# Dense gate and up products with the weight slices as the stationary operand and all 256 tokens streaming

## The chip, the cores and the metric

The kernel runs on one core of a Trainium2 chip. The metric is the device time of one execution in microseconds (us). Three runs of the kernel before gave 1444.27 us as their median, from 1444.11 to 1446.06 us. TensorE (PE) has a granted clock that the profile shows as a share of 2.4 GHz.

## What is computed

A decoder trunk of two layers on 256 tokens with 1024 features: an mLSTM layer with a dense SwiGLU, then a latent attention layer with eight experts of which each token takes two. The change lies in the dense SwiGLU of the first layer:

```python
def swiglu(h, w_gate_up, w_down):
    g, u = jnp.split(h @ w_gate_up, 2, axis=-1)
    return (jax.nn.silu(g) * u) @ w_down

hf = rms_norm(x, ffn_norm[l])
x = x + swiglu(hf, dense_w_gate_up[l // 2], dense_w_down[l // 2])
```

Here `h` is 256 x 1024, `w_gate_up` 1024 x 7168 and `w_down` 3584 x 1024. The root mean square of a token is a factor of its row of `h`, so it may be applied behind the gate and up products. The gain of the norm is put on the normed side before them.

## The kernel before

All products are made in float32 as three passes of fp32r operands: each operand is split into a high part (a rounded copy, `whi`, `xhi`, `hhi`) and a low part (the rest, `wlo`, `xlo`, `hlo`), and high x high, high x low and low x high are summed in PSUM. ScalarE (ACT) makes the high parts of the weights from a ring of six slots in SBUF that SyncE's DMAs fill (`hi_of`), VectorE (DVE) makes the low parts (`lo_of`). Three cuts of split weights are held at a time (`CUTS`). A cut is 2048 columns wide on 128 partitions, and `through` counts the cuts that PE has finished with. `highs` and `lows` count the finished halves of the split.

The dense SwiGLU goes in `NB` = 14 blocks of 256 hidden features (`FB`). A block has two cuts of gate and up weights, one for each half of the 1024 input features (`gate_up`), and one cut of down weights (`down`). `gate_up` takes a slice of 128 features x 128 tokens of `xhi` or `xlo` as the stationary operand (`lhsT`) and streams 512 weight columns: 256 of gate, then 256 of up. With 8 slices of features, 2 tiles of tokens (`t`) and 3 passes that is 48 matmuls of 512 columns for a block, 24 for each cut. The result has tokens on the partitions, in two PSUM banks, one for each token tile. ACT then applies silu to the gate half with the token's factor `rx` as its scale (two instructions of 256 columns, into `sil`), and DVE multiplies the up half by `rx` and by `sil` (two instructions, into `hn`).

`down` needs the hidden features on the partitions. So `turn_hidden` makes four PE transposes of 128 x 128 for a block into a PSUM bank of their own, ACT copies them rounded into `hhi`, and DVE puts the rest into `hlo`. `down` then makes 24 matmuls of 512 columns that sum into PSUM banks 4 to 7.

The order of the work is written by hand, and each engine runs its own program in its order. On PE it is, for a block b in the loop: `gate_up(b)`, `down(b-1)`, `turn_hidden(b)`. Two blocks are one iteration of a hardware loop with five iterations, the first two and the last two blocks stand outside it. In the last block, the transposes stand in the middle of `down(12)`. On ACT and DVE, `block(b)` is: the split of the cuts of `cut_item(b)`, silu or the product, the split of the cut `next_item(b)`, then the split of the hidden features. In block 13 the split of `next_item` is that of the first cut of the next stage (`dkv.0`). `gate_up(0)` has an order of its own, pass by pass, since the normed rows arrive in four pairs of slices (`x1_high`, `x1_low`). On DVE a chain of small instructions for the rotary angles (from `posf` on) stands between `norm("x1")`, which gives `rx`, and block 0.

Of the kernel before, what the change touches and what calls it, by code (L numbers as in the profile page):

```python
# [18 lines left out]
ALU = mybir.AluOpType  # L19
# [7 lines left out]
P = 128  # L27
# [9 lines left out]
def build(nc, T, out):  # L37
# [117 lines left out]
    with ExitStack() as ctx:  # L155
# [108 lines left out]
        hn = carve(NT * FB, NT, FB)  # L264
        silE, hnE = carve(0, EB)[0:CAP], carve(NT * FB, EB)[0:CAP]
# [441 lines left out]
        def _(act):  # L707
# [47 lines left out]
            def block(b, r=None):  # L755

                for n in cut_item(b):
                    hi_of(n, r)
                act.wait_ge(S("through"), count(r, 3, FFN0 + gu_item(b) + 2))
                for t in range(NT):  # L760
                    last = nc.scalar.activation(sil[:, t], PS[:, gu_bank(b) + t, 0:FB], ACT.Silu, scale=rx[:, t:t + 1])
                last.then_inc(S("silu"), 1)
                if next_item(b) < PER:
                    hi_of(next_item(b), r)
                else:
                    front_hi(item["dkv.0"])
                act.wait_ge(S("h_turned"), count(r, 1, b + 1))
                nc.scalar.activation(hidden(b)[0], PS[:, turn_bank(b), :].rearrange("p (a s) -> p a s", a=2), ACT.Copy).then_inc(S("h_high"), 1)
# [146 lines left out]
            nc.scalar.activation(gt, gt, ACT.Exp, scale=-1.0).then_inc(S("gate_exp"), 1)  # L915
            act.wait_ge(S("gate_exp"), 1)
            nc.scalar.activation(gt, gt, ACT.Ln, bias=1.0).then_inc(S("gate_exp"), 1)
# [8 lines left out]
            nc.scalar.activation(gem, gm, ACT.Exp, scale=-1.0).then_inc(S("gate_em"), 1)  # L926
# [218 lines left out]
        def _(pe):  # L1145
# [182 lines left out]
            pe.wait_ge(S("gate_em"), 1)  # L1328
# [77 lines left out]
            def gate_up(b, r=None, between=None):  # L1406

                for h in range(2):
                    if h == 1 and between:
                        between()  # L1410
                    n = gu_item(b) + h
                    j = (FFN0 + n) % CUTS
                    if b == 0:
                        parts = [(k, h * KH + k, t, slice(t * P, (t + 1) * P)) for k in range(KH) for t in range(NT)]
                        pe.wait_ge(S("highs"), FFN0 + n + 1)
                        for k, kx, t, x_ in parts:
                            if k % 2 == 0 and t == 0:
                                pe.wait_ge(S("x1_high"), kx // 2 + 1)
                            mm(PS[:, t, :], lhsT=xhi[:, kx, x_], rhs=whi[:, j, k * W:(k + 1) * W], start=(kx == 0), stop=False)
                        pe.wait_ge(S("lows"), FFN0 + n + 1)  # L1420
                        for k, kx, t, x_ in parts:
                            mm(PS[:, t, :], lhsT=xhi[:, kx, x_], rhs=wlo[:, j, k * W:(k + 1) * W], start=False, stop=False)
                        for k, kx, t, x_ in parts:
                            if k % 2 == 0 and t == 0:
                                pe.wait_ge(S("x1_low"), kx // 2 + 1)
                            last = mm(PS[:, t, :], lhsT=xlo[:, kx, x_], rhs=whi[:, j, k * W:(k + 1) * W], start=False, stop=(kx == KD - 1))
                        last.then_inc(S("through"), 1)
                        continue
                    pe.wait_ge(S("lows"), count(r, 3, FFN0 + n + 1))
                    for k in range(KH):  # L1430
                        for t in range(NT):
                            x_ = slice(t * P, (t + 1) * P)
                            last = three(PS[:, gu_bank(b) + t, :], xhi[:, h * KH + k, x_], xlo[:, h * KH + k, x_], whi[:, j, k * W:(k + 1) * W],
                                         wlo[:, j, k * W:(k + 1) * W], h == 0 and k == 0, h == 1 and k == KH - 1)
                    last.then_inc(S("through"), 1)
# [50 lines left out]
            down(NB - 2, tiles=(1,))  # L1486
# [93 lines left out]
            pe.wait_ge(S("masks_r"), 4)  # L1580
# [200 lines left out]
        def _(dve):  # L1781
# [32 lines left out]
            def block(b, r=None):  # L1814

                for n in cut_item(b):
                    lo_of(n, r)
                dve.wait_ge(S("silu"), count(r, 1, b + 1))
                for t in range(NT):
                    last = v.scalar_tensor_tensor(out=hn[:, t], in0=PS[:, gu_bank(b) + t, FB:2 * FB], scalar=rx[:, t:t + 1], in1=sil[:, t],  # L1820
                                                  op0=ALU.mult, op1=ALU.mult)
                last.then_inc(S("h_ready"), 1)
                if next_item(b) < PER:
                    lo_of(next_item(b), r)
                else:
# [226 lines left out]
            dve.wait_ge(S("gate_exp"), 2)  # L2052
# [82 lines left out]
            norm("x1")  # L2135

# [307 lines left out]
```

## Time and profile before

| | |
|---|---|
| median of 3 runs | 1444.27 us |
| the profiled execution | 1444.03 us |
| its span (first to last instruction) | 1442.3 us |
| PE busy | 99% of the span |
| DVE busy | 79% |
| ACT busy | 67% |
| POOL (GpSimd) busy | 7% |
| dense SwiGLU, first matmul to the first transpose of the next stage | 139.97 to 375.13 us of the span |

The profile's times count from the first instruction. A matmul's row shows its start and a modelled end. Matmuls overlap in the array, so the time that one takes from the engine is read from the distance between starts. PEld is PE's weight load, which runs beside the matmul ahead of it.

### The profile page before, as it was taken

The numbers are of one execution on the slowest core, as the hardware profiler recorded it, in microseconds if no ns is written. First come the engines' busy times: TensorE is split into PE (matmuls) and PEld (weight loads), VectorE is DVE, ScalarE is ACT, GpSimd is POOL, SyncE is SP. The second block draws the span as 40 slices with busy tenths as digits, with TensorE's granted clock in tenths as the row PEclk, the third lists the DMA queues.
The fourth block names the chain that finished last, engine by engine and source line by source line (L and its number), as shares of the span: only waits on it lengthen the run. The fifth ranks groups of instructions, "written<-read, shape, count | busy, mean of one in ns | idle before, by whom it ended". The sixth has DMA issues, their size and how long they took to land.

```text
span 1442.3 us, 19828 instructions
## 1 busy us (share of the span) xinstructions
PE 1434.5 (99%) x6848; PEld 1206.7 (84%) x6848; DVE 1140.7 (79%) x896; ACT 963.9 (67%) x839; POOL 98.7 (7%) x146
## 2 busy tenths in 40 slices
PE   8999999999999999999999999999999999999999
PEld 8898888888998888888888888888888888888887
DVE  6566655454676599989888898898998898888897
ACT  7555443434694577777777777777777777777775
POOL 3010000000032110000000000000000000000100
PEclk9999999999999899999999999999999999999999
DMA  9534655554345599999999999999999999999995
GB/s 335 199 117 146 207 202 175 194 184 147 115 175 160 206 363 390 375 372 395 391 362 394 388 364 383 395 369 377 393 375 367 393 391 349 397 393 370 380 393 203
DMA packets 212591, 442.92 MB, mean 307 GB/s; under 512 B 16373, under 2 KB 56761, under 8 KB 212545
## 3 DMA queue, kind: packets, MB, share of 16 engines
q1 hardware_dynamic: 208640, 430.18, 82.1%
q0 software_dynamic: 3888, 12.13, 2.8%
q8 instruction: 28, 0.46, 0.1%
q14 instruction: 19, 0.15, 0.0%
q10 hardware_dynamic: 16, 0.00, 0.0%
HBM read 434.88 MB, written 7.37 MB: 307 GB/s over the span
## 4 chain that ended last, share of the span: by engine, by line
PE 99%; DVE 0%; ACT 0%; issue 0%; POOL 0%; POOLq 0%; DVEq 0%; ACTq 0%
PE PS L1698 21%; PE PS L1699 21%; PE PS L1702 21%; PE PS L1404 5%; PE PS L1402 5%; PE PS L1403 5%; PE PS L1149 4%; PE PS L1202 2%; PE PS L1197 2%; PE PS L1199 2%; PE PS L1253 1%; PE PS L1259 1%; PE PS L1256 1%; PE PS L1179 1%; PE PS L1687 1%; PE PS L1690 1%
## 5 line engine op out<-in xcount | busy, mean ns | idle before, releaser
L1844 DVE TENSOR_TENSOR wlo<-ring,whi 128x2048 fp32r<-128x2048 f32 x334 | 764.1, 2292 | 96.4 <-ACT whi L784 94.4
L784 ACT ACTIVATE whi<-ring 128x2048 fp32r<-128x2048 f32 x334 | 640.5, 1919 | 186.5 <-PE PS L1702 175.3
L1698 PE MATMUL PS<-whi,xhi 128*128 128x512 f32 x864 | 340.8, 394 | 0.0
L1699 PE MATMUL PS<-whi,xlo 128*128 128x512 f32 x864 | 336.6, 390 | 0.0
L1702 PE MATMUL PS<-wlo,xhi 128*128 128x512 f32 x864 | 231.0, 389 | 0.0
L1702 PEld LDWEIGHTS PS<-wlo,xhi 128*128 128x128 f32 x864 | 162.1, 188 | 33.9 <-DVE wlo L1844 0.2
L1699 PEld LDWEIGHTS PS<-whi,xlo 128*128 128x128 f32 x864 | 162.4, 188 | 32.4
L1698 PEld LDWEIGHTS PS<-whi,xhi 128*128 128x128 f32 x864 | 162.3, 188 | 32.4
L1698 PE MATMUL PS<-whi,hhi 128*128 128x512 f32 x440 | 171.9, 391 | 0.0
L1699 PE MATMUL PS<-whi,hlo 128*128 128x512 f32 x440 | 171.3, 389 | 0.0
L1811 DVE TENSOR_TENSOR wlo<-ring,whi 128x2048 fp32r<-128x2048 f32 x42 | 96.2, 2291 | 59.0 <-ACT whi L753 59.0
L1702 PE MATMUL PS<-wlo,hhi 128*128 128x512 f32 x440 | 117.8, 390 | 0.0
L753 ACT ACTIVATE whi<-ring 128x2048 fp32r<-128x2048 f32 x42 | 80.5, 1916 | 46.3 <-PE PS L1404 37.8
L1702 PEld LDWEIGHTS PS<-wlo,hhi 128*128 128x128 f32 x440 | 82.6, 188 | 17.2
L1699 PEld LDWEIGHTS PS<-whi,hlo 128*128 128x128 f32 x440 | 82.6, 188 | 17.0
L1698 PEld LDWEIGHTS PS<-whi,hhi 128*128 128x128 f32 x440 | 82.6, 188 | 16.9
L1402 PE MATMUL PS<-whi,xhi 128*128 128x512 f32 x224 | 88.3, 394 | 0.0
L1404 PE MATMUL PS<-whi,xlo 128*128 128x512 f32 x224 | 87.3, 390 | 0.0
L1403 PE MATMUL PS<-wlo,xhi 128*128 128x512 f32 x224 | 87.2, 389 | 0.0
L809 ACT ACTIVATE arena<-PS 128x512 f32<-128x512 f32 x56 | 33.5, 599 | 46.2 <-PE PS L1702 46.2
L1977 DVE TENSOR_TENSOR wlo<-ring,whi 128x1536 fp32r<-128x1536 f32 (+4 forms) x28 | 49.3, 1771 | 14.7 <-ACT whi L842 14.7
L1149 PE MATMUL PS<-ident,arena 128*128 128x128 f32 (+3 forms) x378 | 55.7, 272 | 0.0
(377 smaller groups left out, 1586.8 us busy)
## 6 DMA issues: line engine op xcount, KB each, us to landing
ring<-in_moe_w_gate_up SPq DMA_DIRECT2D x448, 512.0 KB, 6.8
ring<-in_moe_w_down SPq DMA_DIRECT2D x224, 512.0 KB, 6.7
ring<-in_dense_w_gate_up SPq DMA_DIRECT2D x56, 512.0 KB, 4.2
ring<-in_dense_w_down SPq DMA_DIRECT2D x28, 512.0 KB, 4.2
ring<-in_a_w_in SPq DMA_DIRECT2D x12, 768.0 KB, 7.1
ring<-in_mem_w_kv SPq DMA_DIRECT2D x4, 1024.0 KB, 5.3
ring<-in_a_w_out SPq DMA_DIRECT2D x4, 1024.0 KB, 4.9
ring<-in_b_w_out SPq DMA_DIRECT2D x4, 1024.0 KB, 5.0
```

Of the source, the lines that this page charges most:

```text
L753: nc.scalar.activation(whi[:, (FFN0 + n) % CUTS, :], ring[:, h * SLOT:(h + 1) * SLOT], ACT.Copy).then_inc(S("highs"), 1)
L784: nc.scalar.activation(whi[:, j, :], ring[:, h * SLOT:(h + 1) * SLOT], ACT.Copy).then_inc(S("highs"), 1)
L1149: return nc.tensor.transpose(dst, src, ident[0:src.shape[0], 0:src.shape[0]])
L1402: mm(out_, lhsT=xh, rhs=wh, start=first, stop=False)
L1403: mm(out_, lhsT=xh, rhs=wl, start=False, stop=False)
L1404: return mm(out_, lhsT=xl, rhs=wh, start=False, stop=last)
L1698: mm(out_, lhsT=xh, rhs=whi[:, j, c0:c0 + HD], start=begin, stop=False)
L1699: mm(out_, lhsT=xl, rhs=whi[:, j, c0:c0 + HD], start=False, stop=False)
L1702: last = mm(out_, lhsT=xh, rhs=wlo[:, j, c0:c0 + HD], start=False, stop=end)
L1811: v.tensor_tensor(wlo[:, j, :], ring[:, h * SLOT:(h + 1) * SLOT], whi[:, j, :].bitcast(F32), ALU.subtract).then_inc(S("lows"), 1)
L1844: v.tensor_tensor(wlo[:, j, :], ring[:, h * SLOT:(h + 1) * SLOT], whi[:, j, :].bitcast(F32), ALU.subtract).then_inc(S("lows"), 1)
L1977: last = v.tensor_tensor(lo, src, hi.bitcast(F32), ALU.subtract)
```

## The change

Gate and up products: the stationary operand is now a slice of 128 features x 128 weight columns of `whi` or `wlo`, and all 256 tokens of `xhi` or `xlo` stream past it. A cut has 4 slices of features, gate and up (`g`), two halves of 128 columns (`c`) and three passes: 48 matmuls of 256 columns where there were 24 of 512. The result has hidden features on the partitions and tokens in the columns, gate in one PSUM bank and up in the other. `turn_hidden` and its four transposes are gone.

The factor `rx` is then needed along the columns. DVE makes two diagonal matrices with `rx` (`rx_diag`), PE multiplies them by a matrix of ones into PSUM behind `gate_up(0)`, and DVE copies the 256 columns into `rx_rows`. In a block, DVE multiplies gate and up from PSUM by `rx_rows` into SBUF (`gs`, `us`, one instruction of 512 columns each), ACT applies silu to `gs` (one of 512 columns), DVE multiplies the two (`hn2`, 512 columns), ACT copies the product rounded into `hhi` (from SBUF, and behind a wait for `down(b-1)`, which reads the same tile), and DVE puts the rest into `hlo`. `gate_up` waits for `h_ready` of the block before from block 2 on. In the last block but one, `down(12)` is in one piece. Three semaphores of the gates of the first layer are merged into `gate_in`.

```diff
@@ gate_up
+                    def out_of(g, c):
+                        return PS[:, gu_bank(b) + g, c * SEQ:(c + 1) * SEQ]
+
+                    parts = [(k, h * KH + k, g, c, slice(k * W + g * FB + c * P, k * W + g * FB + (c + 1) * P))
+                             for k in range(KH) for g in range(2) for c in range(2)]
...
+                    if h == 0 and b > 1:
+                        pe.wait_ge(S("h_ready"), count(r, 1, b))
                     pe.wait_ge(S("lows"), count(r, 3, FFN0 + n + 1))
-                    for k in range(KH):
-                        for t in range(NT):
-                            x_ = slice(t * P, (t + 1) * P)
-                            last = three(PS[:, gu_bank(b) + t, :], xhi[:, h * KH + k, x_], xlo[:, h * KH + k, x_], whi[:, j, k * W:(k + 1) * W],
-                                         wlo[:, j, k * W:(k + 1) * W], h == 0 and k == 0, h == 1 and k == KH - 1)
+                    for k, kx, g, c, w_ in parts:
+                        mm(out_of(g, c), lhsT=whi[:, j, w_], rhs=xhi[:, kx, :], start=(kx == 0 and c == 0), stop=False, skip_group_check=True)
+                        mm(out_of(g, c), lhsT=whi[:, j, w_], rhs=xlo[:, kx, :], start=False, stop=False, skip_group_check=True)
+                        last = mm(out_of(g, c), lhsT=wlo[:, j, w_], rhs=xhi[:, kx, :], start=False, stop=(kx == KD - 1), skip_group_check=True)
                     last.then_inc(S("through"), 1)
@@ PE's order
-            def turn_hidden(b, r=None):
-
-                pe.wait_ge(S("h_ready"), count(r, 1, b + 1))
-                for kk in range(2):
-                    for t in range(NT):
-                        last = tr(PS[:, turn_bank(b), kk * SEQ + t * P:kk * SEQ + (t + 1) * P], hn[:, t, kk * P:(kk + 1) * P])
-                last.then_inc(S("h_turned"), 1)
-
             gate_up(0)
+            pe.wait_ge(S("masks_r"), 4)
+            for t in range(NT):
+                last = mm(PS[:, 4, t * P:(t + 1) * P], lhsT=ones[:, :], rhs=rx_diag[:, t], start=True, stop=True)
+            last.then_inc(S("gains_t"), 1)
             pe.wait_ge(S("x1_low"), 4)
-            gate_up(1, between=lambda: turn_hidden(0))
+            gate_up(1)
             down(0)
-            turn_hidden(1)
             with pe.Fori(0, len(REST)) as r:
                 for b in (2, 3):
                     gate_up(b, r)
                     down(b - 1, r)
-                    turn_hidden(b, r)
             gate_up(NB - 2)
             down(NB - 3)
-            turn_hidden(NB - 2)
             gate_up(NB - 1)
-            down(NB - 2, tiles=(0,))
-            turn_hidden(NB - 1)
-            down(NB - 2, tiles=(1,))
+            down(NB - 2)
             down(NB - 1)
@@ DVE's block(b)
+                dve.wait_ge(S("through"), count(r, 3, FFN0 + gu_item(b) + 2))
+                for g, dst, done in ((0, gs, "g_scaled"), (1, us, "h_ready")):
+                    v.tensor_tensor(dst, PS[:, gu_bank(b) + g, :].rearrange("p (a s) -> p a s", a=2), over(rx_rows, 2), ALU.mult).then_inc(S(done), 1)
+                dve.wait_ge(S("h_ready"), count(r, 1, b + 1))
                 dve.wait_ge(S("silu"), count(r, 1, b + 1))
-                for t in range(NT):
-                    last = v.scalar_tensor_tensor(out=hn[:, t], in0=PS[:, gu_bank(b) + t, FB:2 * FB], scalar=rx[:, t:t + 1], in1=sil[:, t],
-                                                  op0=ALU.mult, op1=ALU.mult)
-                last.then_inc(S("h_ready"), 1)
+                v.tensor_tensor(hn2, us, sil2, ALU.mult).then_inc(S("h_turned"), 1)
@@ ACT's block(b)
-                act.wait_ge(S("through"), count(r, 3, FFN0 + gu_item(b) + 2))
-                for t in range(NT):
-                    last = nc.scalar.activation(sil[:, t], PS[:, gu_bank(b) + t, 0:FB], ACT.Silu, scale=rx[:, t:t + 1])
-                last.then_inc(S("silu"), 1)
+                act.wait_ge(S("g_scaled"), count(r, 1, b + 1))
+                nc.scalar.activation(sil2, gs, ACT.Silu).then_inc(S("silu"), 1)
...
+                if 0 < b < NB - 1:
+                    act.wait_ge(S("through"), count(r, 3, FFN0 + dn_item(b - 1) + 1))
+                nc.scalar.activation(hidden(b)[0], hn2, ACT.Copy).then_inc(S("h_high"), 1)
@@ DVE, between norm("x1") and the rotary angles
             norm("x1")
+            dve.wait_ge(S("scaled"), nidx["x1"] + 1)
+            for t in range(NT):
+                last = v.tensor_scalar(rx_diag[:, t], ident[:, :], rx[:, t:t + 1], None, ALU.mult)
+            last.then_inc(S("masks_r"), 1)
+            dve.wait_ge(S("gains_t"), 3)
+            then(v.tensor_copy(rx_rows, PS[:, 4, 0:SEQ]))
```

PE's program in the first block before: six passes of `gate_up(0)` (L1419 to L1426), then `gate_up(1)`.

```order
368 L1419 MATMUL PS<-whi,xhi 128x512 x8
369 L1422 MATMUL PS<-wlo,xhi 128x512 x8
370 L1426 MATMUL PS<-whi,xlo 128x512 x8
...
374 L1402 MATMUL PS<-whi,xhi 128x512
375 L1403 MATMUL PS<-wlo,xhi 128x512
376 L1404 MATMUL PS<-whi,xlo 128x512
```

The same place now. L1472 are the two products with the matrix of ones.

```order
368 L1425 MATMUL PS<-xhi,whi 128x256 x16
369 L1428 MATMUL PS<-xhi,wlo 128x256 x16
370 L1432 MATMUL PS<-xlo,whi 128x256 x16
...
374 L1472 MATMUL PS<-arena,ones 128x128 x2
375 L1439 MATMUL PS<-xhi,whi 128x256
376 L1440 MATMUL PS<-xlo,whi 128x256
377 L1441 MATMUL PS<-xhi,wlo 128x256
```

Each pass has twice the matmuls at half the width, the operands have changed sides, and two small matmuls stand between the blocks.

PE's program at the end of the hardware loop's iteration before: the last matmuls of `down`, then `turn_hidden` (L1149) and the branch back.

```order
599 L1402 MATMUL PS<-whi,hhi 128x512
600 L1403 MATMUL PS<-wlo,hhi 128x512
601 L1404 MATMUL PS<-whi,hlo 128x512
602 L1464 REGISTER_ALU
603 L1149 MATMUL PS<-ident,arena 128x128 x4
604 L1475 REGISTER_ALU
605 L1475 COMPARE_AND_BRANCH
```

The same place now.

```order
741 L1406 MATMUL PS<-whi,hhi 128x512
742 L1407 MATMUL PS<-wlo,hhi 128x512
743 L1408 MATMUL PS<-whi,hlo 128x512
744 L1477 REGISTER_ALU
745 L1477 COMPARE_AND_BRANCH
```

The four transposes are gone, and `down` is followed by the branch.

DVE's program before, from `rx` on (L1802) through the rotary angles to block 0 (from L1811 on; L1820 is the product into `hn`, L1828 the rest `hlo`).

```order
80 L1802 COPY rx<-rstd 128x2
81 L2147 CAST posf<-posi 128x2
82 L2149 TENSOR_SCALAR rot<-invf,posf 128x32 x2
...
90 L2160 TENSOR_SCALAR rot<-rot 128x64
91 L1811 TENSOR_TENSOR wlo<-ring,whi 128x2048
92 L1820 SCALAR_TENSOR_TENSOR arena<-PS,rx,arena 128x256 x2
93 L1811 TENSOR_TENSOR wlo<-ring,whi 128x2048
94 L1828 TENSOR_TENSOR hlo<-PS,hhi 128x512
```

The same place now (L2136 makes `rx_diag`, L2139 copies `rx_rows`, L1818 makes `gs` and `us`, L1821 `hn2`).

```order
80 L1800 COPY rx<-rstd 128x2
81 L2136 TENSOR_SCALAR arena<-ident,rx 128x128 x2
82 L2139 COPY arena<-PS 128x256
83 L2151 CAST posf<-posi 128x2
84 L2153 TENSOR_SCALAR rot<-invf,posf 128x32 x2
...
93 L1809 TENSOR_TENSOR wlo<-ring,whi 128x2048
94 L1818 TENSOR_TENSOR arena<-PS,arena 128x512 x2
95 L1821 TENSOR_TENSOR arena<-arena 128x512
96 L1809 TENSOR_TENSOR wlo<-ring,whi 128x2048
97 L1827 TENSOR_TENSOR hlo<-arena,hhi 128x512
```

Three instructions stand ahead of the rotary angles, one of which waits for PE, and a block has four instructions of 512 columns beside the splits, where it had two of 256 and one of 512.

## Rows read from the trace of the kernel before

**Rows 1.** The page: the span, and each engine's busy time, share and instructions.
```profile
span 1442.3 us, 19828 instructions
PE 1434.5 (99%) x6848; PEld 1206.7 (84%) x6848; DVE 1140.7 (79%) x896; ACT 963.9 (67%) x839; POOL 98.7 (7%) x146
```

**Rows 2.** Windows of the span: length, busy time by engine, clock, DMA share, GB/s.
```profile
139.97:375.13 235.16, 235.16 (x1066) 194.72 (x1065) 126.56 (x116) 103.25 (x103) 2.24 (x2) 1.00 0.54 178
...
471.00:481.30 10.30, 10.18 (x64) 9.47 (x62) 5.89 (x18) 4.54 (x8) 1.95 (x4) 0.79 0.33 127
```

**Rows 3.** Groups by line and form, PE, 139.9 to 375.13 us.
```profile
L1402 PE MATMUL PS<-whi,xhi 128*128 128x512 f32 x216 | 85.2, 395 | 0.0
...
L1149 PE MATMUL PS<-ident,arena 128*128 128x128 f32 x56 | 8.4, 272 | 0.0
L1419 PE MATMUL PS<-whi,xhi 128*128 128x512 f32 x16 | 4.1, 395 | 0.0
```

**Rows 4.** Timeline of PE, one block: start us, us, engine, line, operation, tiles.
```profile
224.70 0.39 PE L1402 MATMUL PS<-whi,xhi 128*128 128x512 f32 x1
...
234.90 0.60 PE L1149 MATMUL PS<-ident,arena 128*128 128x128 f32 x4
235.26 0.48 PE L1402 MATMUL PS<-whi,xhi 128*128 128x512 f32 x1
...
236.04 0.39 PE L1402 MATMUL PS<-whi,xhi 128*128 128x512 f32 x1
...
251.69 0.60 PE L1149 MATMUL PS<-ident,arena 128*128 128x128 f32 x4
```

**Rows 5.** Timeline of PE behind the dense stage: matmuls of 384, then 256 columns.
```profile
388.46 0.33 PE L1197 MATMUL PS<-whi,xhi 128*128 128x384 f32 x1
...
391.06 0.33 PE L1199 MATMUL PS<-whi,xlo 128*128 128x384 f32 x1
...
393.30 0.29 PE L1197 MATMUL PS<-whi,xhi 128*128 128x256 f32 x1
...
396.78 0.28 PE L1199 MATMUL PS<-whi,xlo 128*128 128x256 f32 x1
```

**Rows 6.** Timeline of PE: an output product whose matmuls share stationary slices in pairs.
```profile
466.88 1.07 PE L1253 MATMUL PS<-whi,xhi 128*128 128x512 f32 x4
...
469.60 1.03 PE L1149 MATMUL PS<-ident,xres 128*128 128x128 f32 x8
```

**Rows 7.** Timeline of DVE, then of ACT, then of PE in the first block.
```profile
148.40 0.17 DVE L1802 COPY rx<-rstd 128x2 f32<-128x2 f32 x1 [0.92 <-POOL rstd L613]
148.48 0.17 DVE L2147 CAST posf<-posi 128x2 f32<-128x2 int32 x1
...
151.53 2.28 DVE L1811 TENSOR_TENSOR wlo<-ring,whi 128x2048 fp32r<-128x2048 f32 x1
...
148.61 1.92 ACT L753 ACTIVATE whi<-ring 128x2048 fp32r<-128x2048 f32 x1 [2.72 <-DVE rx L1802]
...
139.97 2.08 PE L1419 MATMUL PS<-whi,xhi 128*128 128x512 f32 x8
```

**Rows 8.** Groups by line: elementwise instructions on 512 and 256 columns.
```profile
L1804 DVE TENSOR_TENSOR arena<-arena,rstd 128x512 f32<-128x512 f32 x3 | 2.1, 692 | 5.9 <-POOL rstd L613 5.9
...
L716 ACT ACTIVATE arena<-arena 128x512 f32<-128x512 f32 x1 | 0.6, 624 | 0.0
...
L2006 DVE TENSOR_SCALAR memv<-PS,rm 128x256 f32<-128x256 f32 x4 | 1.8, 480 | 3.5 <-ACT arena L859 3.5
```

**Rows 9.** Timeline of PE, ACT and DVE in the last block.
```profile
363.78 0.39 PE L1402 MATMUL PS<-whi,hhi 128*128 128x512 f32 x1
...
369.69 0.39 PE L1402 MATMUL PS<-whi,xhi 128*128 128x512 f32 x1
...
364.71 1.92 ACT L842 ACTIVATE whi<-ring,gains 128x320 fp32r<-128x320 f32 x4
...
366.65 1.94 DVE L1979 SCALAR_TENSOR_TENSOR wlo<-ring,gains,whi 128x320 fp32r<-128x320 f32 x4 [0.93 <-ACT whi L842]
```

More of the change, by code:

```diff
@@ L264, in build @@
         hn = carve(NT * FB, NT, FB)
+        gs, us = carve(2 * NT * FB, 2, SEQ), carve(3 * NT * FB, 2, SEQ)
+        rx_rows = carve(4 * NT * FB, SEQ)
+        rx_diag = carve(4 * NT * FB + SEQ, NT, P)
+        sil2, hn2 = carve(0, 2, SEQ), carve(NT * FB, 2, SEQ)
         silE, hnE = carve(0, EB)[0:CAP], carve(NT * FB, EB)[0:CAP]
@@ L767, in block @@
                 act.wait_ge(S("h_turned"), count(r, 1, b + 1))
-                nc.scalar.activation(hidden(b)[0], PS[:, turn_bank(b), :].rearrange("p (a s) -> p a s", a=2), ACT.Copy).then_inc(S("h_high"), 1)
+                if 0 < b < NB - 1:
+                    act.wait_ge(S("through"), count(r, 3, FFN0 + dn_item(b - 1) + 1))
+                nc.scalar.activation(hidden(b)[0], hn2, ACT.Copy).then_inc(S("h_high"), 1)
             def dense():
@@ L914, in _ @@
             act.wait_ge(S("gate_steps"), 1)
-            nc.scalar.activation(gt, gt, ACT.Exp, scale=-1.0).then_inc(S("gate_exp"), 1)
-            act.wait_ge(S("gate_exp"), 1)
-            nc.scalar.activation(gt, gt, ACT.Ln, bias=1.0).then_inc(S("gate_exp"), 1)
+            nc.scalar.activation(gt, gt, ACT.Exp, scale=-1.0).then_inc(S("gate_in"), 1)
+            act.wait_ge(S("gate_in"), 3)
+            nc.scalar.activation(gt, gt, ACT.Ln, bias=1.0).then_inc(S("gate_in"), 1)
             front_hi(7)
@@ L925, in _ @@
             act.wait_ge(S("gate_steps"), 2)
-            nc.scalar.activation(gem, gm, ACT.Exp, scale=-1.0).then_inc(S("gate_em"), 1)
+            nc.scalar.activation(gem, gm, ACT.Exp, scale=-1.0).then_inc(S("gate_in"), 1)
             front_hi(9)
@@ L1327, in _ @@
             pe.wait_ge(S("v_out"), 1)
-            pe.wait_ge(S("gate_em"), 1)
+            pe.wait_ge(S("gate_in"), 5)
             for r, src in enumerate((ga, gem)):
@@ L1404, in three, with gate_up @@
                 return mm(out_, lhsT=xl, rhs=wh, start=False, stop=last)
-            def gate_up(b, r=None, between=None):
+            def gate_up(b, r=None):
                 for h in range(2):
-                    if h == 1 and between:
-                        between()
                     n = gu_item(b) + h
                     j = (FFN0 + n) % CUTS
+                    def out_of(g, c):
+                        return PS[:, gu_bank(b) + g, c * SEQ:(c + 1) * SEQ]
+                    parts = [(k, h * KH + k, g, c, slice(k * W + g * FB + c * P, k * W + g * FB + (c + 1) * P))
+                             for k in range(KH) for g in range(2) for c in range(2)]
@@ L1413, in gate_up @@
                     if b == 0:
-                        parts = [(k, h * KH + k, t, slice(t * P, (t + 1) * P)) for k in range(KH) for t in range(NT)]
                         pe.wait_ge(S("highs"), FFN0 + n + 1)
-                        for k, kx, t, x_ in parts:
-                            if k % 2 == 0 and t == 0:
+                        for k, kx, g, c, w_ in parts:
+                            if k % 2 == 0 and g + c == 0:
                                 pe.wait_ge(S("x1_high"), kx // 2 + 1)
-                            mm(PS[:, t, :], lhsT=xhi[:, kx, x_], rhs=whi[:, j, k * W:(k + 1) * W], start=(kx == 0), stop=False)
+                            mm(out_of(g, c), lhsT=whi[:, j, w_], rhs=xhi[:, kx, :], start=(kx == 0 and c == 0), stop=False, skip_group_check=True)
@@ L1420, in gate_up @@
                         pe.wait_ge(S("lows"), FFN0 + n + 1)
[L1421 to L1424, printed above, removed]
+                        for k, kx, g, c, w_ in parts:
+                            mm(out_of(g, c), lhsT=wlo[:, j, w_], rhs=xhi[:, kx, :], start=False, stop=False, skip_group_check=True)
@@ L1425, in gate_up @@
+                        for k, kx, g, c, w_ in parts:
+                            if k % 2 == 0 and g + c == 0:
                                 pe.wait_ge(S("x1_low"), kx // 2 + 1)
-                            last = mm(PS[:, t, :], lhsT=xlo[:, kx, x_], rhs=whi[:, j, k * W:(k + 1) * W], start=False, stop=(kx == KD - 1))
+                            last = mm(out_of(g, c), lhsT=whi[:, j, w_], rhs=xlo[:, kx, :], start=False, stop=(kx == KD - 1), skip_group_check=True)
                         last.then_inc(S("through"), 1)
@@ L1428, in gate_up @@
                         continue
+                    if h == 0 and b > 1:
+                        pe.wait_ge(S("h_ready"), count(r, 1, b))
                     pe.wait_ge(S("lows"), count(r, 3, FFN0 + n + 1))
-                    for k in range(KH):
-                        for t in range(NT):
-                            x_ = slice(t * P, (t + 1) * P)
-                            last = three(PS[:, gu_bank(b) + t, :], xhi[:, h * KH + k, x_], xlo[:, h * KH + k, x_], whi[:, j, k * W:(k + 1) * W],
-                                         wlo[:, j, k * W:(k + 1) * W], h == 0 and k == 0, h == 1 and k == KH - 1)
+                    for k, kx, g, c, w_ in parts:
+                        mm(out_of(g, c), lhsT=whi[:, j, w_], rhs=xhi[:, kx, :], start=(kx == 0 and c == 0), stop=False, skip_group_check=True)
+                        mm(out_of(g, c), lhsT=whi[:, j, w_], rhs=xlo[:, kx, :], start=False, stop=False, skip_group_check=True)
+                        last = mm(out_of(g, c), lhsT=wlo[:, j, w_], rhs=xhi[:, kx, :], start=False, stop=(kx == KD - 1), skip_group_check=True)
@@ L1578, in attend @@
                 return last
-            pe.wait_ge(S("masks_r"), 4)
+            pe.wait_ge(S("masks_r"), 5)
             pe.wait_ge(S("kq_even"), 4)
@@ L1827, in block @@
                 dve.wait_ge(S("h_high"), count(r, 1, b + 1))
-                v.tensor_tensor(hidden(b)[1], PS[:, turn_bank(b), :].rearrange("p (a s) -> p a s", a=2), hidden(b)[0].bitcast(F32),
-                                ALU.subtract).then_inc(S("h_low"), 1)
+                v.tensor_tensor(hidden(b)[1], hn2, hidden(b)[0].bitcast(F32), ALU.subtract).then_inc(S("h_low"), 1)
             def dense():
@@ L2051, in _ @@
             front_lo(6)
-            dve.wait_ge(S("gate_exp"), 2)
+            dve.wait_ge(S("gate_in"), 4)
             then(v.tensor_tensor(glf, gf, gt, ALU.subtract))
```

## The prediction

> **What bounds the kernel now.** I read the page's first section, then the windows of the dense stage, then the timeline of one block. PE is busy for 99% of the span [rows 1] and for all 235.16 us of the dense stage, at full clock [rows 2]; DVE is busy there for 127 us and ACT for 103. So in this stage the time is the sum of what PE's instructions take from each other, and DVE and ACT count only where PE comes to wait for them. Only this stage is changed, and the rest should keep its time.
>
> What a matmul takes is the distance of starts. In the block that ends with the transposes at 234.90, the 45 matmuls of 512 columns from 224.70 on take 10.20 us [rows 4]: 226.7 ns each. The block repeats after 251.69 - 234.90 = 16.79 us [rows 4], and 72 x 226.7 ns = 16.32 us of it are matmuls. The four transposes take the other 0.47 us: 0.36 to the next matmul, and 0.10 to 0.12 more as it and the ones behind it come late (236.04 - 234.90 = 1.14 us for four transposes and three matmuls of 0.227). The whole stage agrees: (216 + 16) x 3 = 696 matmuls with `xhi` or `xlo`, of which 24 are the last `down`, so 672 of gate and up; with 14 downs of 24 that is 1008 matmuls x 226.7 ns = 228.5 us, and 56 transposes [rows 3], 14 x 0.47 = 6.6 us, make 235.1 of 235.16.
>
> **Part one: the transposes go.** 14 x 0.47 = 6.6 us less on PE. All of it lay on the bounding engine.
>
> **Part two: 672 matmuls of 512 columns become 1344 of 256.** The same columns stream, so what counts is whether a matmul has a fixed part. The trace has the new form: matmuls of 256 fp32r columns, each with its own weight load and pairs that sum into one place in PSUM. From 393.30 to 396.78 there are 29 steps in 3.48 us: 120.0 ns each [rows 5]. With 384 columns, 15 steps in 2.60 us give 173.3 ns [rows 5]. So 120.0, 173.3 and 226.7 lie on one line: columns at 2.4 GHz (106.7, 160, 213.3) and 13.3 ns beside them. Splitting a matmul in two pays the 13.3 ns again: 672 x 13.3 ns = 9.0 us more. A second weight load of 128 columns fits: the 256-column rows have one for each matmul and keep the line. The transposes, of 128 columns each with its load, start 0.11 us apart (four take 0.60 us, the last of them 0.27, so three steps take 0.33), just under the 120 ns.
>
> Here a rule speaks against this reading. The Trainium skill (TensorE: Matmul & The Clock Gate, Back-to-back issue gap) gives a warm matmul columns / 2.4 GHz plus 2.5 ns. By it the split would cost 672 x 2.5 = 1.7 us, not 9.0, and the sum below would come out 7.3 us lower, at 1440.9. The trace measures 13.3 ns at three widths, and I go by the trace.
>
> Could sharing the stationary slice save something? Now two neighbours (`whi` against `xhi`, then `xlo`) use one slice of `whi`. In the output product at 466.88 the two neighbours of each pair share a slice of `xhi` too, and 12 matmuls take 2.72 us to 469.60, or 226.7 ns each [rows 6]. Nothing is saved.
>
> Parts one and two together: 9.0 - 6.6 = **2.4 us more**. In a block, 24 x 226.7 + 96 x 120 = 16.96 us instead of 16.79.
>
> **Part three: two matmuls with ones.** Two of 128 columns behind `gate_up(0)`. Nearest are the transposes: half of their 0.47 us is 0.24. They are ordinary float32 and no transposes, so up to twice that. I take 0.35 us.
>
> **Part four: DVE waits for these in the first block.** Before, the rotary chain runs on DVE from 148.48 to 151.53, 3.05 us, while PE is in `gate_up(0)`, and the split of cut 3 follows at once for 2.28 us [rows 7]. Now DVE's copy of `rx_rows` waits for PE's two matmuls, and the chain and the split are queued behind it. `gate_up(0)` starts at 139.97 [rows 7] and its 96 matmuls of 120 ns end at 151.5; the ones come to about 151.9 to 152.0; the copy of 256 columns from PSUM takes some 0.45 (0.48 for a like one [rows 8]), to 152.4; the chain ends at 155.5, the split of cut 3 at 157.8. PE has the first half of `gate_up(1)`, 48 x 120 ns = 5.76 us, from 151.85 to 157.6, and then needs that cut. With its weight load behind the wait, it goes on at about 158.05: **0.45 us** lost. Then DVE has `gs` (0.69, as a like instruction [rows 8]) to 158.5 and `us` to 159.1; silu on ACT (0.62 [rows 8]) ends at 159.1, `hn2` at 159.8; ACT's split of cut 4, which before came early, follows silu and ends at 161.0 (1.92 as in [rows 7]); DVE's half ends at 163.3, and `hlo` at 163.9. PE has finished `gate_up(1)` at 163.8 and needs both for `down(0)`: **0.3 us** lost, so 0.75 with the first. The bounds are 0 (each step 0.3 us faster than I read it) and 2 us. A block later the cuts are 3 us ahead again.
>
> **Part five: the loop.** Behind the end of a gate_up at T: `gs` T+0.7, silu T+1.35, `hn2` T+2.0, ACT's next cut T+3.3, DVE's T+5.6, high part of the hidden features T+6.05 (behind `down(b-1)`, at T+5.4), low part T+6.8. `down(b)` needs that at T+17. The next cuts come at T+10.3, needed at T+17. `us` at T+1.4 frees the PSUM banks, needed at T+5.4. PE waits for none: 10 us of cover. DVE gets some 1.2 us more a block (two of 0.69 and one more against 0.88), ACT loses 0.2; both idle anyway.
>
> **Part six: the last block.** Here only `down(12)` covers the chain. Counted from its first matmul D (363.78 before; `down(13)` began at 369.69, D+5.91 [rows 9]): now the last gate and up matmul ends at D+0.16, `gs` at D+0.85, silu at D+1.5. ACT's and DVE's splits of the next stage's first cut take 1.92 and 1.94 [rows 9] in front of the hidden features' own: D+3.4 and D+5.35, then `xlo` D+6.0, and the first matmul at about D+6.15. PE is through with `down(12)` at D+5.44. So **0.65 us** lost (bounds 0 and 1).
>
> **Sum.** 2.4 + 0.35 + 0.75 + 0.65 = 4.15 us, on the profiled execution's 1444.03: **1448.2 us**. The median, 1444.27, lies 0.24 above that execution, which is within the runs' own spread of 2 us. 0.2% or 2.9 us is about what a measurement here can tell from no change, so the line between the same and slower is 1447.2.
>
> **Rivals.** (a) The fixed part doesn't double: part of the 13.3 ns belongs to a change of PSUM bank or of operands that comes half as often now. For it: two neighbours now share a stationary slice, and four in a row a bank. Against it: [rows 5] and [rows 6]. At the full 9.0 us it gives 1439.2, faster; it decides the sign from 5.8 ns on: 672 x 5.8 ns is the 3.9 us between my forecast and the time before. The skill's gap above is a case of this rival, between that and my forecast. Chance 0.06.
>
> (b) The covers hold: my chains in parts four and six are each some tenths too long, and PE waits nowhere. That gives 2.4 + 0.35, 1446.8: the same. For it: every wait here is the small difference of two sums of 6 us. Against: DVE's wait for PE is new, and the chain behind it can't go earlier. Chance 0.24.
>
> (c) PE can't keep 120 ns. The longest such stretch before is 48 matmuls in one piece; now each block has 96, with two instructions each, and two blocks make a loop whose body grows from 152 to 240 pairs. 3 ns a matmul would give 4.0 us, 1452.2. For it: no long stretch shows it. Against: the branch back costs nothing that can be seen at 226.7 ns, since the period is the same with and without it. Chance 0.10.
>
> (d) Shifted by 4 us, the stretches with half clock near 471 us, where the tokens are routed, fall differently. They can move the time by 1 to 2 us either way; this widens the range and has no sign.
>
> **How the numbers follow.** The forecast has 0.60, (a) 0.06, (b) 0.24, (c) 0.10. The forecast and (b) reach with their bounds and (d) from 1445.5 to 1450.5; half of (c) takes it to 1451. Faster by over 0.2%: 0.05. Within 0.2%: (b), the low end of the forecast and a bit of (a), 0.30. Slower: 0.65.
>
> **What would show it.** In the profile after: gate and up matmuls 120 ns apart and a block period of 16.96 us (120 ns wrong: part two; 110 ns is rival (a)); no transposes in the dense stage; idle time of PE of some 0.4 us ahead of cut 3 and 0.3 ahead of `down(0)`, released by DVE, and 0.65 ahead of `down(13)`; the stage from 139.97 to about 379.3. A weight load that reads 128 columns of `whi` at a slower pace than those of `xhi`, or a difference outside the stage, would prove me wrong.

## The result, and the profile after

| | before | after |
|---|---|---|
| median of 20 runs | 1444.07 us | 1447.75 us |
| lowest to highest | 1442.06 to 1446.06 | 1446.05 to 1449.8 |
| the profiled execution | 1444.03 | 1448.08 |
| its span | 1442.3 | 1446.3 |

The ratio is 1.0025 with a 95% interval from 1.0019 to 1.0031: 3.7 us or a quarter of a percent slower. The forecast was 1448.2 us.

The new page's head answers to [rows 1]. PE has 620 matmuls more (672 from the split, 4 for the ones, less 56 transposes) and stays busy for 99%.

```profile
span 1446.3 us, 21098 instructions
PE 1437.5 (99%) x7468; PEld 1235.4 (85%) x7468; DVE 1157.0 (80%) x913; ACT 961.3 (66%) x825; POOL 99.1 (7%) x146
```

I cut each span at four matmuls of PE: the first gate and up matmul, the first transpose of the next stage, the first router matmul and the first expert matmul.

| profiled execution, us | before | after | change |
|---|---|---|---|
| to the first gate and up matmul | 139.97 | 140.30 | +0.33 |
| dense stage | 235.16 | 239.65 | +4.49 |
| to the first router matmul | 98.83 | 98.90 | +0.07 |
| routing, to the first expert matmul | 14.68 | 13.74 | -0.94 |
| experts to the end | 953.66 | 953.71 | +0.05 |
| span | 1442.3 | 1446.3 | +4.0 |

So the change costs 4.5 us where it was made, and 0.9 us come back 100 us later, in a stretch that it doesn't touch. The 0.33 us ahead of the stage is no part of the change either: among the kernels below, that stretch ends anywhere from 139.5 to 141.9 us.

The groups by line and form of PE in the dense stage, which answer to [rows 3]: 416 matmuls of 256 columns for each pass, and 32 for each in block 0, 1344 in all. The transposes are gone.

```profile
L1439 PE MATMUL PS<-xhi,whi 128*128 128x256 f32 x416 | 117.9, 283 | 0.1
L1441 PE MATMUL PS<-xhi,wlo 128*128 128x256 f32 x416 | 117.8, 283 | 0.0
L1440 PE MATMUL PS<-xlo,whi 128*128 128x256 f32 x416 | 117.7, 283 | 0.0
...
L1425 PE MATMUL PS<-xhi,whi 128*128 128x256 f32 x32 | 4.2, 285 | 0.0
```

The timeline of PE in the first block after (start us, us, engine, line, operation, tiles; `x4` merges four records, and the bracket gives the idle time ahead of an instruction and what ended it):

```profile
140.30 2.15 PE L1425 MATMUL PS<-xhi,whi 128*128 128x256 f32 x16
...
151.88 0.61 PE L1472 MATMUL PS<-arena,ones 128*128 128x128 f32 x4
...
152.45 0.28 PE L1440 MATMUL PS<-xlo,whi 128*128 128x256 f32 x1
...
157.96 0.28 PE L1441 MATMUL PS<-xhi,wlo 128*128 128x256 f32 x1
158.38 0.39 PE L1439 MATMUL PS<-xhi,whi 128*128 128x256 f32 x1
158.60 0.28 PE L1440 MATMUL PS<-xlo,whi 128*128 128x256 f32 x1
...
164.12 0.28 PE L1441 MATMUL PS<-xhi,wlo 128*128 128x256 f32 x1
164.47 0.47 PE L1406 MATMUL PS<-whi,hhi 128*128 128x512 f32 x1
164.78 0.40 PE L1407 MATMUL PS<-wlo,hhi 128*128 128x512 f32 x1
```

From 152.45 to 157.96 there are 46 steps in 5.51 us, 119.8 ns each. The two products with ones are four matmul records, and with them and the late first matmul behind them 0.45 us pass (152.45 - 151.88 less one step). The step to cut 3 takes 0.42 us in place of 0.12 and the next 0.22: 0.40 us lost. The step to `down(0)` takes 0.35 in place of 0.12 and the next 0.31 in place of 0.23: 0.31 us lost. The weight load at the first of these places names DVE's split of cut 3:

```profile
158.38 0.19 PEld L1439 LDWEIGHTS PS<-xhi,whi 128*128 128x128 f32 x1 [0.34 <-DVE wlo L1809]
```

The one at `down(0)` names no releaser; DVE's `hlo` below ends at 164.32, 0.15 us ahead of the matmul. DVE's timeline at that place shows the queue that the prediction described: the copy, the chain, then the splits of cut 3 and cut 4, then `hlo`.

```profile
152.53 0.42 DVE L2139 COPY arena<-PS 128x256 f32<-128x256 f32 x1 [3.10 <-PE PS L1472]
...
156.04 2.28 DVE L1809 TENSOR_TENSOR wlo<-ring,whi 128x2048 fp32r<-128x2048 f32 x1
158.24 1.28 DVE L1818 TENSOR_TENSOR arena<-PS,arena 128x512 f32<-128x512 f32 x2
...
161.43 2.29 DVE L1809 TENSOR_TENSOR wlo<-ring,whi 128x2048 fp32r<-128x2048 f32 x1 [1.04 <-ACT whi L757]
163.64 0.68 DVE L1827 TENSOR_TENSOR hlo<-arena,hhi 128x512 fp32r<-128x512 f32 x1
```

The timeline of PE in the loop (two first matmuls of `down`, one block apart) and in the last block:

```profile
232.48 0.40 PE L1406 MATMUL PS<-whi,hhi 128*128 128x512 f32 x1
...
249.46 0.40 PE L1406 MATMUL PS<-whi,hhi 128*128 128x512 f32 x1
...
373.56 0.39 PE L1408 MATMUL PS<-whi,hlo 128*128 128x512 f32 x1
374.42 0.47 PE L1406 MATMUL PS<-whi,xhi 128*128 128x512 f32 x1 [0.47 <-DVE xlo L1827]
374.72 0.40 PE L1407 MATMUL PS<-wlo,xhi 128*128 128x512 f32 x1
...
379.95 1.91 PE L1153 MATMUL PS<-ident,xres 128*128 128x128 f32 x16
```

The block takes 16.98 us (16.79 before [rows 4]). Ahead of `down(13)` 0.86 us pass in place of 0.23, and then 0.30: 0.71 us lost. The row names `xlo` on DVE as the releaser, the chain of part six.

The stage adds up: 1344 x 0.120 + 336 x 0.2267 = 237.44; with 0.45, 0.40, 0.31 and 0.71 it is 239.31; the last 0.3 us I put down to the changes between the two widths, 0.02 us a block.

### The profile page after: what moved, and what is told of

The parts are those of the page before. It is cut to its first block, busy times and chain, and to the rows that moved or that the text cites. A ratio compares the mean times of both kernels' runs of the same rounds, so it can differ in the third digit from the quotient of the medians.

```text
span 1446.3 us, 21098 instructions
## 1 busy us (share of the span) xinstructions
PE 1437.5 (99%) x7468; PEld 1235.4 (85%) x7468; DVE 1157.0 (80%) x913; ACT 961.3 (66%) x825; POOL 99.1 (7%) x146
## 4 chain that ended last, share of the span: by engine, by line
PE 98%; DVE 1%; issue 0%; ACT 0%; POOL 0%; POOLq 0%; DVEq 0%; ACTq 0%
PE PS L1696 21%; PE PS L1697 20%; PE PS L1700 20%; PE PS L1153 4%; PE PS L1439 3%; PE PS L1441 3%; PE PS L1440 3%; PE PS L1206 2%; PE PS L1201 2%; PE PS L1203 2%; PE PS L1406 2%; PE PS L1407 2%; PE PS L1408 2%; PE PS L1257 1%; PE PS L1260 1%; PE PS L1263 1%
## 5 line engine op out<-in xcount | busy, mean ns | idle before, releaser
L1696 PE MATMUL PS<-whi,xhi 128*128 128x512 f32 x864 | 340.9, 395 | 0.0
L1697 PE MATMUL PS<-whi,xlo 128*128 128x512 f32 x864 | 336.6, 390 | 0.0
L1700 PE MATMUL PS<-wlo,xhi 128*128 128x512 f32 x864 | 231.0, 389 | 0.0
L1439 PE MATMUL PS<-xhi,whi 128*128 128x256 f32 x416 | 117.9, 283 | 0.1
L1441 PE MATMUL PS<-xhi,wlo 128*128 128x256 f32 x416 | 117.8, 283 | 0.0
L1440 PE MATMUL PS<-xlo,whi 128*128 128x256 f32 x416 | 117.7, 283 | 0.0
L1439 PEld LDWEIGHTS PS<-xhi,whi 128*128 128x128 f32 x416 | 79.8, 192 | 0.8 <-DVE wlo L1809 0.3
L1440 PEld LDWEIGHTS PS<-xlo,whi 128*128 128x128 f32 x416 | 79.8, 192 | 0.5
L1441 PEld LDWEIGHTS PS<-xhi,wlo 128*128 128x128 f32 x416 | 79.8, 192 | 0.0
```

The lines of the kernel that those rows point to most:

```text
L1439: mm(out_of(g, c), lhsT=whi[:, j, w_], rhs=xhi[:, kx, :], start=(kx == 0 and c == 0), stop=False, skip_group_check=True)
L1440: mm(out_of(g, c), lhsT=whi[:, j, w_], rhs=xlo[:, kx, :], start=False, stop=False, skip_group_check=True)
L1441: last = mm(out_of(g, c), lhsT=wlo[:, j, w_], rhs=xhi[:, kx, :], start=False, stop=(kx == KD - 1), skip_group_check=True)
L1696: mm(out_, lhsT=xh, rhs=whi[:, j, c0:c0 + HD], start=begin, stop=False)
L1697: mm(out_, lhsT=xl, rhs=whi[:, j, c0:c0 + HD], start=False, stop=False)
L1700: last = mm(out_, lhsT=xh, rhs=wlo[:, j, c0:c0 + HD], start=False, stop=end)
```

## The experiments

Each ran beside the kernel before on the same chip, whose median there was 1444.1 us (1443.7 beside the single transposes in the experts and the narrower matmuls). The ratio is that to this median. The table of all of them, cut at the same four matmuls:

| profiled execution, us | dense stage | routing | median | ratio to before, interval |
|---|---|---|---|---|
| before | 235.16 | 14.68 | 1444.1 | |
| after | 239.65 | 13.74 | 1447.75 | 1.0025 [1.0019, 1.0031] |
| split alone | 243.94 | 13.06 | 1450.96 | 1.0046 [1.0032, 1.0060] |
| transposes twice | 241.29 | 14.69 | 1449.91 | 1.0037 [1.0024, 1.0051] |
| after, waits covered | 238.22 | 14.68 | 1447.03 | 1.0017 [1.0008, 1.0026] |
| single transposes, dense | 236.92 | 13.06 | 1444.4 | 1.0001 [0.9992, 1.0010] |
| single transposes, experts too | 236.91 | 13.29 | 1447.55 | 1.0029 [1.0018, 1.0039] |
| 13 matmuls added | 236.75 | 13.26 | 1444.79 | 1.0004 [0.9995, 1.0013] |
| 26 matmuls added | 238.31 | 14.68 | 1446.95 | 1.0019 [1.0010, 1.0028] |
| narrower matmuls, one run | 250.93 | 13.64 | 1460.69 | |

**The split alone.**

```diff
-                            last = three(PS[:, gu_bank(b) + t, :], xhi[:, h * KH + k, x_], xlo[:, h * KH + k, x_], whi[:, j, k * W:(k + 1) * W],
-                                         wlo[:, j, k * W:(k + 1) * W], h == 0 and k == 0, h == 1 and k == KH - 1)
+                            halves(out_, xh, wh, h == 0 and k == 0, False)
+                            halves(out_, xh, wl, False, False)
+                            last = halves(out_, xl, wh, False, h == 1 and k == KH - 1)
```

> The kernel before, with the split alone: xhi and xlo stay the stationary side, and each of the 672 gate and up matmuls of 512 columns is made as two of 256 that share their stationary slice. Transposes and all else stay. My theory (a fixed 13.3 ns for each matmul, whichever side is stationary): steps of 120 ns, 9.0 us more than before, 1453.1 us. The rival (the fixed part belongs to the change of the stationary slice or doesn't double): steps of 107 to 113 ns, 0 to 5 us more.

The stage took 8.8 us more than before, 9.0 expected. The timeline of PE in this kernel, two rows with 26 steps between them in 3.12 us, 120.0 ns each:

```profile
229.37 0.40 PE L1409 MATMUL PS<-wlo,xhi 128*128 128x256 f32 x2
...
232.49 0.40 PE L1409 MATMUL PS<-whi,xlo 128*128 128x256 f32 x2
```

So the 120 ns belong to the width. They are the same with `xhi` as the stationary side as with `whi`, and here, too, each pair shares its stationary slice. The total was 6.8 us more, not 9.0: routing took 1.6 us less. That was no part of either theory and led to the last two kernels.

**The transposes twice.**

```diff
-                for kk in range(2):
+                for again in range(2):
...
```

> The kernel before, with each block's four transposes made twice in a row. My theory (the transposes lie whole on PE's path, 0.11 us each while a row of them lasts): 14 x 4 x 0.11 = 6.1 us more, 1450.2 us. A rival (part of the 0.47 us that I gave to a block's transposes is a change between kinds of work that is paid once, and an edge of less than 0.2 us for each group): under 5 us more.

The stage took 6.13 us more, 0.109 us for each of the 56 added transposes, and the median was 5.8 us higher. A row of eight in the timeline, then the next matmul:

```profile
236.68 1.03 PE L1149 MATMUL PS<-ident,arena 128*128 128x128 f32 x8
237.47 0.48 PE L1402 MATMUL PS<-whi,xhi 128*128 128x512 f32 x1
237.78 0.39 PE L1403 MATMUL PS<-wlo,xhi 128*128 128x512 f32 x1
```

Transposes lie on PE's path whole, at 0.108 us each (the row of eight: 1.03 less 0.27 us for seven steps). Of the 0.47 us of a block's four, 0.04 us is an edge, which goes with them. The rival, under 5 us, is refuted.

**The changed kernel with its waits covered.**

```diff
@@ DVE
             last.then_inc(S("masks_r"), 1)
-            dve.wait_ge(S("gains_t"), 3)
-            then(v.tensor_copy(rx_rows, PS[:, 4, 0:SEQ]))
...
+            dve.wait_ge(S("gains_t"), 3)
+            then(v.tensor_copy(rx_rows, PS[:, 4, 0:SEQ]))
             dense()
@@ ACT's block(b), and the same on DVE with front_lo
-                else:
-                    front_hi(item["dkv.0"])
                 act.wait_ge(S("h_turned"), count(r, 1, b + 1))
...
                 nc.scalar.activation(hidden(b)[0], hn2, ACT.Copy).then_inc(S("h_high"), 1)
+                if next_item(b) >= PER:
+                    front_hi(item["dkv.0"])
```

> The changed kernel, with the waits covered: on DVE the rotary chain runs before the copy of rx_rows, and in block 13 ACT and DVE split the hidden features before the next stage's first cut. My theory (the stalls ahead of cut 3, of down(0) and of down(13) are those two queues): no idle time of PE at these three places, 1.1 to 1.4 us less than the changed kernel, 1446.5 us, so that 2.4 to 2.9 us more than before is left. The rival (the stalls have another cause, or a later wait takes their place): 1447.7 us.

The stage took 238.22 us, 1.43 less than the changed kernel's 239.65. The three waits that I read off there add up to 0.40 + 0.31 + 0.71 = 1.42. All three are gone; the timeline at `down(0)` and at `down(13)`:

```profile
163.52 0.28 PE L1441 MATMUL PS<-xhi,wlo 128*128 128x256 f32 x1
163.64 0.40 PE L1406 MATMUL PS<-whi,hhi 128*128 128x512 f32 x1
...
372.64 0.39 PE L1408 MATMUL PS<-whi,hlo 128*128 128x512 f32 x1
372.87 0.39 PE L1406 MATMUL PS<-whi,xhi 128*128 128x512 f32 x1
```

The median fell by only 0.7 us, to 1447.03, between the 1446.5 of the theory and the 1447.7 of the rival; the rows decide for the theory. In the profiled executions routing took 14.68 us again in place of 13.74, so 0.94 of the 1.43 went back there. What is left over before, 3.1 us of stage, is the split less the transposes, the ones and the changes of width: 2.4 + 0.45 + 0.3.

**Single transposes.** Since a row of transposes costs 0.11 us each, and the four cost 6.6 us in all, I tried to make them cheaper in the kernel before, which would beat both.

```diff
+                            if turn is not None and u >= 0:
+                                turn_one(turn, r, u)
+                            u += 1
                             last = three(PS[:, 4 + 2 * t + hh, :], hhi[:, kk, x_], hlo[:, kk, x_], whi[:, j, c0:c0 + HD],
```

> The kernel before, but a block's four transposes stand one by one between groups of three wide matmuls of the down product instead of in a row. My theory (a row of transposes is held to 0.11 us each by their weight loads, and one that stands alone has its load hidden under a 512-column matmul and pays 128 columns and the fixed part, 0.067 us): 14 x (0.47 - 0.27) = 2.8 us less than before, 1441.3 us. The rival (a transpose costs 0.11 us wherever it stands): 0 to 0.5 us less.

The theory fell: 2.8 us less was expected, and the stage took 1.76 us more. The timeline of PE around one of them:

```profile
232.42 0.39 PE L1406 MATMUL PS<-whi,hlo 128*128 128x512 f32 x1
232.65 0.27 PE L1151 MATMUL PS<-ident,arena 128*128 128x128 f32 x1
232.68 0.48 PE L1404 MATMUL PS<-whi,hhi 128*128 128x512 f32 x1
232.99 0.40 PE L1405 MATMUL PS<-wlo,hhi 128*128 128x512 f32 x1
...
233.46 0.27 PE L1151 MATMUL PS<-ident,arena 128*128 128x128 f32 x1
...
250.31 0.27 PE L1151 MATMUL PS<-ident,arena 128*128 128x128 f32 x1
```

The matmul behind the transpose starts 0.03 us after it, but the next comes 0.31 us later, not 0.227: the price is only moved. From one transpose to the next with three matmuls between them it is 0.81 us (from 232.65 to 233.46), 0.13 for the transpose. The block takes 16.85 us (250.31 - 233.46) in place of 16.79, 0.8 us for 14 blocks. And in the last block the hidden features came later, and PE waited 0.8 us for `xlo`:

```profile
371.55 0.47 PE L1404 MATMUL PS<-whi,xhi 128*128 128x512 f32 x1 [0.81 <-DVE xlo L1831]
```

The median, 1444.4, is about that of before; in the profiled execution routing was 1.62 us shorter.

The same in the experts:

```diff
+                    if turn is not None:
...
+                        turned = tr(PS[:, 3, c * CAP:(c + 1) * CAP], hnE[:, c * P:(c + 1) * P])
...
                     mm(out_, lhsT=xh, rhs=whi[:, j, c0:c0 + HD], start=begin, stop=False)
```

> As the kernel with single transposes in the dense stage, and the same in the experts: the four transposes of a block's hidden features stand one by one between the pairs of matmuls of the down product, in 55 of the 56 expert blocks. My theory: 0.2 us less for each, 11 us more off, 1430.3 us. The rival (the experts are held by the weight transfers, whose share of the DMA engines is full in that stage, or the split of the weights on DVE comes late): 1441 us, no more than the dense stage gives.

Neither theory holds, since both expected less time. The experts took 957.3 us in place of 953.7, 3.6 us more. Some 1.1 us of it are two waits of PE for DVE, each met once, that before doesn't have (0.8 us ahead of a transpose, 0.3 behind a split of weights). The rest is 0.045 us for each of the 55 blocks. PE shows no wait for a weight transfer there; a single transpose is dearer than one in a row there too.

**Narrower matmuls.** Blocks 12 and 13 of the kernel before were cut finer, in a single run made for its trace.

```diff
+                                cuts = (0, 128, 256, 384, 512) if b == NB - 2 else (0, 192, 384, 512)
...
+                                    for c0, c1 in zip(cuts, cuts[1:]):
+                                        last = mm(out_[:, c0:c1], lhsT=x, rhs=w[:, c0:c1], start=(begin and c0 == 0), stop=end, skip_group_check=True)
```

> The kernel before, with the gate and up matmuls of block 12 cut into four of 128 columns, and those of block 13 into 192, 192 and 128. It asks how near the 256-column form is to the floor that the weight loads set. My theory (13.3 ns and the columns, but not under 0.107 us, since each matmul loads 128 columns): 128 columns at 107 to 109 ns in place of 67, 192 columns at 107 to 109 in place of 93; block 12 takes 48 x 4 x 0.108 = 20.7 us of PE for gate and up where it took 10.9. The rival (no floor, only the fixed part): 66.7 and 93.3 ns, 12.8 us.

The timeline of PE, in block 12 (52 steps in 5.81 us) and in block 13 (30 steps in 3.35 us):

```profile
343.73 0.61 PE L1439 MATMUL PS<-wlo,xhi 128*128 128x128 f32 x4
...
349.54 0.61 PE L1439 MATMUL PS<-whi,xlo 128*128 128x128 f32 x4
...
366.28 0.50 PE L1439 MATMUL PS<-whi,xhi 128*128 128x192 f32 x3
...
369.63 0.50 PE L1439 MATMUL PS<-wlo,xhi 128*128 128x192 f32 x3
```

Both are 111.7 ns a step, at either width. The stage agrees: 336 x 111.7 ns less 96 x 226.7 is 15.8 us, and it took 15.8 more than before. So there is a floor, a little higher than the 107 to 109 that I expected, and the 256-column matmul with its 120 ns stands 8 ns above it. That the floor is the weight load of 128 columns fits, since both widths share it, but no run changed the load's size, so this is not shown.

**Added work ahead of routing.** In the changed kernel, the split alone, the single transposes and the narrower matmuls, routing was shorter by 0.9 to 1.6 us, in the others it was not. To see whether that is a matter of when it starts, the last two kernels only put useless matmuls into the dense stage of the kernel before.

```diff
             gate_up(0)
+            keep_warm(6, 13)
             pe.wait_ge(S("x1_low"), 4)
```

> The kernel before, with 13 useless matmuls of 256 columns behind gate_up(0): PE gets 1.6 us more in the dense stage, and nothing else changes. Theory that the routing stretch behind the attention gives or takes time by where it falls against the stretch of half clock: the stage is 1.6 us longer, the half clock lasts 6.8 us in place of 10.2, the stretch from the first router matmul to the experts is 1 to 1.6 us shorter, and the total is 0 to 0.6 us over before, about 1444.4 us. The rival (what is put on PE's path is paid in full): 1445.7 us.

> The same with 26 of them: PE gets 3.1 us more in the dense stage. Theory that the place against the half clock counts: the routing starts 3.1 us later and the half clock lasts 10.2 us again, so the whole 3.1 us is paid, about 1447.2 us, 2.8 us over the kernel with 13 for half as much again of added work. The rival: 1447.2 us too, but 1.6 us over the kernel with 13.

The stage took 1.59 and 3.15 us more. With 13, routing took 13.26 us in place of 14.68, and the profiled span was 1442.3 us, the same as before (the stage also began 0.16 us earlier). With 26, routing took 14.68 again and the span was 1445.2. The windows from 475 to 496 us of before, of the kernel with 13 and of the one with 26 (length, busy by engine, granted clock, DMA share, GB/s):

```profile
475.00:496.00 21.00, 21.00 (x114) 19.74 (x112) 12.49 (x25) 7.80 (x9) 3.01 (x6) 0.76 0.53 188
```
```profile
475.00:496.00 21.00, 21.00 (x126) 19.47 (x127) 12.98 (x26) 8.65 (x10) 3.01 (x6) 0.84 0.53 190
```
```profile
475.00:496.00 21.00, 20.88 (x119) 19.59 (x118) 12.12 (x27) 7.51 (x10) 3.00 (x6) 0.76 0.42 152
```

The mean granted clock over these 21 us is 0.76, 0.84 and 0.76. At the 1.2 GHz level for the missing part that is 10.1, 6.7 and 10.1 us at half clock. The same instructions of PE take longer where it falls. From the second group of router matmuls to the products behind them, before and then with 13:

```profile
475.24 3.59 PE L1632 MATMUL PS<-router,xT 128*128 128x8 f32 x24
...
480.75 0.44 PE L1655 MATMUL PS<-arena,before 128*128 128x16 f32 x2
```
```profile
476.65 2.74 PE L1633 MATMUL PS<-router,xT 128*128 128x8 f32 x24
...
480.96 0.58 PE L1656 MATMUL PS<-arena,before 128*128 128x16 f32 x2
```

These are 5.51 us and 4.31: 1.2 of the 1.42 us.

The medians are 0.7 and 2.9 us over before. The first interval, -0.7 to +1.9 us, holds the rival's 1.6 as well, and the step from 13 to 26, 2.2 us for 1.56 us of work, lies between the theory's 2.8 and the rival's 1.6. So the medians don't decide it.

The mean granted clock of every execution helps. Of 54 executions of before, 40 have 0.995 and 4 have 0.996; with 13 added, all 11 have 0.996; with 26, 5 of 11 have 0.995 and 4 have 0.996. The kernels whose profiled execution had the short routing also have 0.996 most often (after 12 of 20, the split alone 4 of 5, the single transposes 7 of 11 and 5 of 8). So the added work does change how long the half clock lasts. But one kernel differs from execution to execution too: before takes about 1442.0 us at 0.998, 1442.9 at 0.996, 1444.1 at 0.995 and 1445.9 at 0.994. At 0.996 the kernel with 13 is about 1.9 us over before: at equal clock the added work is paid. The three digits of the clock leave up to 0.7 us open in such a comparison.

The window from 475 to 496 us of the changed kernel:

```profile
475.00:496.00 21.00, 20.52 (x125) 18.93 (x124) 13.11 (x29) 7.87 (x11) 3.50 (x7) 0.84 0.47 172
```

## Why the prediction was right

Point by point, in the order of its sum:

- **Parts one and two, 2.4 us.** The prediction had both terms right. The steps are 119.8 to 120.0 ns after and in the kernel with the split alone, and that kernel's stage is 8.8 us longer for 9.0 expected. The transposes went; doubled they cost 6.1 us, 0.108 each, and 0.04 of edge for each four gives the 6.6 that I took off. The block is 16.98 us, 0.02 more than forecast, which is the first few wide matmuls behind narrow ones at 0.23 to 0.24; 0.3 us in all were missing from the sum. By the rule that the Trainium skill gives (TensorE: Matmul & The Clock Gate, Back-to-back issue gap), the split would have cost 1.7 us. The trace disagrees with its 2.5 ns and has 13.3; the section calls the rule that of an isolated matmul, which the prediction left out.
- **Part three, 0.35 us.** It was 0.45. A float32 product that is no transpose stands as two matmuls in the records, so there were four records and not two.
- **Part four, 0.75 us.** It was 0.40 + 0.31 = 0.71, at the two places named. The row names DVE only for the first, but the covered kernel took both away, so the queue behind the copy of `rx_rows` is shown as the cause.
- **Part five.** No wait of PE in the loop.
- **Part six, 0.65 us.** It was 0.71, released by `xlo` as said, and gone in the covered kernel. The part's own times give 0.71 as well: 6.15 less 5.44.
- **The stage.** 4.15 forecast, 4.49 measured. The difference is mostly the 0.3 between the widths.
- **The total.** 4.15 forecast, 4.05 between the profiled executions and 3.7 between the medians. It is nearer than its parts deserve: the 0.3 too little in the stage and 0.33 ahead of it met 0.94 us that routing gave back. That part is luck. It is item (d) among the rivals, which I had given no sign and 1 to 2 us. At equal mean clock, after is 4.2 us over before at 0.998 (1446.2 and 1442.0), 4.8 at 0.996 and 5.4 at 0.995 (4, 12 and 4 executions of after); the 3.7 between the medians is smaller because after has 0.996 more often.

Rival (a), the fixed part doesn't double, is refuted by the split alone. Rival (b), the covers hold, is refuted by the rows of the three waits, and its kernel was then built: 1447.03 us, just at the line that I drew between the same and slower. Rival (c), PE can't keep 120 ns over a long stretch, is refuted by the block period.

## What to carry to other kernels

Before swapping the sides of a product to save transposes, count matmuls: where the array is the bound, each has a fixed part besides its columns, and halving the width doubles it. Here 672 x 13.3 ns against 56 transposes of 0.12 us was a loss of 2.4 us, and it could be read from 45, 29 and 15 steps of a timeline. If the swap also makes a row of factors necessary, put the chain that makes it behind nothing and in front of nothing that the bounding engine will want soon.

A gain or loss of 1 to 2 us in a kernel with a stretch at half clock, whose place and length differ between executions, isn't a verdict on the change. Cut the span at fixed instructions and compare the pieces, and compare executions of equal mean clock.

## What the runs showed of the hardware

- fp32r matmuls that each load 128 weight columns, at full granted clock: 226.7 ns a step at 512 columns, 173.3 at 384, 120.0 at 256, and 111.7 at both 192 and 128. The first three are the columns at 2.4 GHz and 13.3 ns; the last two are a floor. What the 13.3 ns consists of, no run shows.
- A float32 transpose of 128 x 128 costs 0.108 us in a row and 0.12 to 0.13 alone between 512-column matmuls. Its own step looks like 0.03 us there, and the rest shows one step later.
- The half clock in the routing stretch lasts 10.1 or 6.7 us, by kernel and by execution. With 1.6 us of useless matmuls 300 us ahead of it, the profiled execution had the 6.7, and 1.42 us came back. Executions of one kernel, before, took from about 1442.0 us at a mean clock of 0.998 to 1445.9 at 0.994.
